# Host-side layout of the weights, larger DMA runs, and six smaller moves in a decoder-layer kernel

## The reference, cut to what matters

```python
a = rms_norm(h, norm_mix)
z, xbc, dt_raw, uv = split(a @ w_in)            # w_in: 1024 x 2568
y_ssd = gated_norm(ssd_scan(silu(conv(xbc)), softplus(dt_raw + dt_bias), ...), z)
u, v = split(gelu(uv)); y_gm = u * (tril(W_s) @ rms_norm(v) + b)
h = h + concat(y_ssd, y_gm) @ w_out             # 1024 x 1024
for e in range(16):                             # each token uses 2 of the 16 experts
    hid = silu(t @ w_gate[e]) * (t @ w_up[e])   # 1024 x 512 each
    y = y + comb[:, e:e + 1] * (hid @ w_down[e])  # 512 x 1024
h = h + y
h = h + sigmoid(rms_norm(h) @ w_pg) * rms_norm(p @ w_ple)
```

## Time and profile before

| | |
|---|---|
| median of three runs | 1130.89 us (1130.82 to 1131.54) |
| profiled execution: time, span | 1131.93 us, 1130.1 us |
| PE busy | 1057.6 us, 94% of the span |
| DVE, ACT, POOL busy | 700.2, 502.7, 184.1 us |
| DMA, mean | 181 GB/s, 204.82 MB |

### The profile page before, as it was taken

One profiled execution on the slowest core, in us unless ns is written; L12 is line 12 of the kernel. 1 busy time (PEld: TensorE's weight loads), 2 busy tenths in 40 slices (PEclk: granted clock), 3 DMA queues, 4 the chain that ended last, 5 costly groups with the idle time before them and its releaser, 6 DMA issues.

```text
span 1130.1 us, 17444 instructions
## 1 busy us (share of the span) xinstructions
PE 1057.6 (94%) x6221; PEld 912.5 (81%) x6222; DVE 700.2 (62%) x1103; ACT 502.7 (44%) x872; POOL 184.1 (16%) x344
## 2 busy tenths in 40 slices
PE   7999999997999999946999999799999999999896
PEld 5777799985776788745988999798899999878685
DVE  4422575814767667156599467889946753585664
ACT  6733322123111121151589357788935652564332
POOL 3611001100133112111000000000000000065542
PEclk9999999999899999857999999999999999999999
DMA  9701400222512362169399775999977556142441
GB/s 335 233 23 55 170 2 1 75 79 72 164 70 76 120 234 85 56 195 296 141 367 380 266 278 179 381 358 369 380 265 278 181 190 225 53 171 75 169 149 56
DMA packets 131607, 204.82 MB, mean 181 GB/s; under 512 B 11375, under 2 KB 98031, under 8 KB 131434
## 3 DMA queue, kind: packets, MB, share of 16 engines
q1 hardware_dynamic: 121450, 169.82, 44.2%
q0 software_dynamic: 6512, 21.77, 5.4%
q10 hardware_dynamic: 3600, 12.62, 2.8%
HBM read 169.74 MB, written 34.46 MB: 181 GB/s over the span
## 4 chain that ended last, share of the span: by engine, by line
PE 56%; DVE 10%; issue 4%; DMA 3%; ACT 2%; DVEq 1%; POOL 0%; ACTq 0%; SPq 0%; POOLq 0%; another core or an unknown queue 0%
PE bank L608 12%; PE bank L610 11%; PE bank L609 11%; PE bank L602 4%; DVE w_lo L1531 3%; PE bank L852 3%; PE bank L854 3%; PE bank L853 3%; PE bank L596 2%; PE bank L824 1%; PE bank L791 1%; DMA raw_gu<-in_w_up 1%; ACT w_hi L1923 1%; DMA xg<-m_rows,index_u 1%; DMA hx<-h_rows 1%
## 5 line engine op out<-in xcount | busy, mean ns | idle before, releaser
L608 PE MATMUL bank<-w_hi,xh 128*128 128x256 f32 x768 | 220.2, 287 | 2.7 <-DVE xl L1052 2.7
L609 PE MATMUL bank<-w_lo,xh 128*128 128x256 f32 x768 | 218.0, 284 | 0.0
L610 PE MATMUL bank<-w_hi,xl 128*128 128x256 f32 x768 | 218.0, 284 | 0.0
L1531 DVE SCALAR_TENSOR_TENSOR w_lo<-raw_gu,cols,w_hi 128x512 fp32r<-128x512 f32 x264 | 177.9, 746 | 10.9 <-ACT w_hi L1923 9.8
L1923 ACT ACTIVATE w_hi<-raw_gu,cols 128x512 fp32r<-128x512 f32 x264 | 165.4, 714 | 32.1 <-PE bank L610 16.4
L608 PEld LDWEIGHTS bank<-w_hi,xh 128*128 128x128 f32 x768 | 147.7, 192 | 4.2 <-issue 3.1
L609 PEld LDWEIGHTS bank<-w_lo,xh 128*128 128x128 f32 x768 | 147.9, 193 | 0.8
L610 PEld LDWEIGHTS bank<-w_hi,xl 128*128 128x128 f32 x768 | 147.7, 192 | 0.0
L608 PE MATMUL bank<-w_hi,hid_hi 128*128 128x512 f32 x192 | 79.6, 415 | 0.0
L2231 POOL COPY index_u<-token_u 128x1 uint32 (+1 forms) x25 | 6.1, 244 | 434.2 <-PE bank L602 411.5
L609 PE MATMUL bank<-w_lo,hid_hi 128*128 128x512 f32 x192 | 75.9, 395 | 0.0
(11 more groups left out here) (373 smaller groups left out, 2169.2 us busy)
## 6 DMA issues: line engine op xcount, KB each, us to landing
raw_gu<-in_w_gate SPq DMA_DIRECT2D x32, 1024.0 KB, 7.6
raw_gu<-in_w_up SPq DMA_DIRECT2D x32, 1024.0 KB, 10.1
raw_d<-in_w_down SPq DMA_DIRECT2D x16, 2048.0 KB, 11.8
y_rows<-yb ACTq DMA_DIRECT2D x24, 512.0 KB, 6.3
raw_w<-in_w_in SPq DMA_DIRECT2D x20, 512.0 KB, 6.3
xr<-in_x_prompt_t SPq DMA_DIRECT2D x8, 512.0 KB, 9.4
xst<-in_x_prompt SPq DMA_DIRECT2D x8, 512.0 KB, 9.7
raw_o<-in_w_out SPq DMA_DIRECT2D x8, 512.0 KB, 3.5
```

Of the source, the lines that this page charges most:

```text
L608: nc.tensor.matmul(out, lh(k), rh(k), start=(k == 0), stop=False)
L609: nc.tensor.matmul(out, lh(k), rl(k), start=False, stop=False)
L610: last = nc.tensor.matmul(out, ll(k), rh(k), start=False, stop=(k == (K or len(ks)) - 1))
L1531: ins = V.scalar_tensor_tensor(out=gu_lo[:, k, :, cols_], in0=raw_gu[q // KC][:, k, :, :], scalar=gain(e, k), in1=gu_hi[:, k, :, cols_].bi ...
```

## The change

- The host hands over `w_in`, gate and up, down and `w_pg` in the order in which they are loaded, so that a run is 4 KB (`w_in`) or 8 KB (gate, up, down, `w_pg`).
- Gate and up are loaded in four quarters of 1 MB (column half by half of the rows), down in two halves, each as soon as its part of the raw buffer has been split; ACT waits for each part by itself.
- All 16 blocks that could be unused are filled, in the first stage, behind the loads of the third block of `w_in`; the fills after the plan are gone.
- `p_in`, `ps_in` and the `norm_ple` row are loaded ahead of the expert stage; `p_in` has a place of its own.
- In a block `hid_transposes(1, ·)` comes behind the first quarter of down.
- The four low parts of the second half of `w_out` are made by POOL, ahead of its `y_rstd(0)`; ACT does `decay(0)` behind the first of the four high parts. `out_half(0, 0)` and the load of `s_nat` wait for POOL's semaphore `o_low`.

```diff
-                c0 = W_COLS[block]
-                sp.dma_start(raw_w[:, 2 * part:2 * part + 2, :], w_src[:, 2 * part:2 * part + 2, c0:c0 + BANK]
-                             ).then_inc(s(f"w{part}_loaded"), 16)
+                sp.dma_start(raw_w[:, 2 * part:2 * part + 2, :], i["w_in_blocks"][block, part]).then_inc(s(f"w{part}_loaded"), 16)
...
             for part in range(4):
                 w_load(2, part)
+            for b in range(NE, BLOCKS):
+                sp.dma_start(y_rows[b * P:(b + 1) * P, :].rearrange("p (k n) -> p k n", n=P),
+                             ones[:, :].unsqueeze(1).to_broadcast([P, KC, P])).then_inc(s("unused_filled"), 16)
...
-            sp.wait_ge(s("a_split"), KC * 5 + KC)
+            sp.wait_ge(s("o_low"), KC // 2)
...
-                for w, name in enumerate(("w_gate", "w_up")):
-                    sp.dma_start(raw_gu[q][:, :, w, :], i[name][0, bass.ds(e, 1), :, q * HE:(q + 1) * HE].rearrange(
-                        "o (k p) n -> p (o k) n", p=P)).then_inc(s(f"gu{q}_loaded"), 16)
+                sp.dma_start(raw_gu[q][:, part * KC // 2:(part + 1) * KC // 2].rearrange("p k w n -> p (k w n)"),
+                             i["w_gate_up"][bass.ds(e, 1), q, part].rearrange("o p n -> p (o n)")).then_inc(s(f"w{2 * q + part}_loaded"), 16)
...
+                if n == TILES + 1:
+                    sp.wait_ge(s("mTp_done"), TILES)
+                    sp.wait_ge(s("h_stored"), 16 * TILES)
+                    sp.dma_start(p_in, i["p_prompt_t"].rearrange("(k p) t -> p k t", p=P)).then_inc(s("p_loaded"), 16)
+                    sp.dma_start(ple_row, i["norm_ple"].partition_broadcast(P).rearrange("q o n -> q (o n)")).then_inc(s("c_rows_loaded"), 16)
...
-            with sp.If(unused > 0):
-                with sp.Fori(0, unused) as j:
-                    sp.dma_start(y_rows[bass.ds((BLOCKS - 1 - j) * P, P), :].rearrange("p (k n) -> p k n", n=P),
-                                 ones[:, :].unsqueeze(1).to_broadcast([P, KC, P])).then_inc(s("unused_filled"), 16)
...
-                gate_up(e, 0, sp.snap(done - KC - DC))
-                gate_up(e, 1, sp.snap(done - DC))
-                down(e, done)
+                for q in range(2):
+                    for part in range(2):
+                        gate_up(e, q, part, sp.snap(done - DC - (3 - 2 * q - part) * KC // 2))
+                down(e, 0, sp.snap(done - DC // 2))
+                down(e, 1, done)
...
                 b_rows(pe.snap(16 * n + 16))
-                hid_transposes(1, pe.snap(2 * n + 1))
                 pe.wait_ge(s("w_split"), steps + STEPS)
...
                 for quarter in range(4):
                     part, half = quarter // 2, quarter % 2
+                    if quarter == 1:
+                        hid_transposes(1, pe.snap(2 * n + 1))
...
             front(0)
-            for j in range(KC // 2):
-                o_split(1, j)
             weights(0)
...
             bt_evict(0)
-            for j in range(KC // 2):
+            o_high(1, 0)
+            decay(0)
+            for j in range(1, KC // 2):
                 o_high(1, j)
-            decay(0)
...
+            for j in range(KC // 2):
+                pool.wait_ge(s("a_high"), KC * 5 + KC // 2 + j + 1)
+                G.tensor_tensor(wo_lo[1][:, j, :], raw_o[:, j, :], wo_hi[1][:, j, :].bitcast(F32), ALU.subtract).then_inc(s("o_low"), 1)
             for n in range(TILES + 1):
                 if n < TILES:
                     y_rstd(n)
```

More of the change, by code:

```diff
@@ L61, in build @@
     TILES = NT + 1
-    IN = i["w_in"].shape[2]
+    IN = sizes["w_in"][2]
     HEADS = i["dt_bias"].shape[1]
@@ L77, in build @@
     EPG = NE // NG
-    DE = i["w_gate"].shape[3]
+    DE = sizes["w_gate"][3]
     DC = DE // P
@@ L518, in _ @@
                     sp.wait_ge(s("ssm_stored"), 16 * XC)
-                    gate_up(0, 0, None)
-                    gate_up(0, 1, None)
+                    for q in range(2):
+                        for part in range(2):
+                            gate_up(0, q, part, None)
                 if n == TILES:
@@ L525, in _ @@
                     sp.wait_ge(s("out_done"), 2 * TILES)
-                    down(0, None)
+                    for part in range(2):
+                        down(0, part, None)
+                if n == TILES + 1:
[3 more added lines that the diff above has]
+                    sp.dma_start(ple_row, i["norm_ple"].partition_broadcast(P).rearrange("q o n -> q (o n)")).then_inc(s("c_rows_loaded"), 16)
@@ L547, in _ @@
+                down(e, 0, sp.snap(done - DC // 2))
+                down(e, 1, done)
+            sp.wait_ge(s("lg_ready"), TILES)
             sp.dma_start(ps_in, i["p_sample_t"].rearrange("(k p) t -> p k t", p=P)).then_inc(s("p_loaded"), 16)
-            sp.dma_start(ple_row, i["norm_ple"].partition_broadcast(P).rearrange("q o n -> q (o n)")).then_inc(s("c_rows_loaded"), 16)
-            with sp.Fori(NE // 2, NE) as e:
+            with sp.Fori(1, NE) as e:
                 next_expert(e)
             for q in range(2):
[L553 to L556, removed]
+                for part in range(2):
+                    sp.wait_ge(s("w_split"), STEPS * NE - DC - (3 - 2 * q - part) * KC // 2)
+                    sp.dma_start(raw_gu[q][:, part * KC // 2:(part + 1) * KC // 2].rearrange("p k w n -> p (k w n)"),
+                                 i["w_pg_rows"][q, part]).then_inc(s(f"w{2 * q + part}_loaded"), 16)
@@ L557, in _ @@
+            sp.wait_ge(s("w_split"), STEPS * NE - DC // 2)
+            sp.dma_start(raw_d[:, 0:PC, :], i["w_ple"][0].rearrange("(k p) n -> p k n", p=P)).then_inc(s("d0_loaded"), 16)
             sp.wait_ge(s("w_split"), STEPS * NE)
-            sp.dma_start(raw_d[:, 0:PC, :], i["w_ple"][0].rearrange("(k p) n -> p k n", p=P)).then_inc(s("d_loaded"), 16)
             sp.dma_start(fin_row, i["norm_final"].partition_broadcast(P)).then_inc(s("c_rows_loaded"), 16)
@@ L1916, in split @@
                 x2 = isinstance(e, int)
-                if at[0] != "D":
-                    act.wait_ge(s(f"gu{int(at[0] == 'B')}_loaded"), 32 * (e + 1) if x2 else act.snap(32 * e + 32))
+                loads = {q * KC // 2: (f"w{q}_loaded", 7) for q in range(4)}
+                loads.update({2 * KC + q * DC // 2: (f"d{q}_loaded", 0) for q in range(2)})
                 steps = SPLITS[at]
                 for q in steps:
+                    if q in loads:
+                        name, earlier = loads[q]
+                        act.wait_ge(s(name), 16 * (e + earlier + 1) if x2 else act.snap(16 * e + 16 * earlier + 16))
                     if q < 2 * KC:
@@ L1951, in final_pg @@
             def final_pg(half, k):
-                if k == 0:
-                    act.wait_ge(s(f"gu{half}_loaded"), 32 * (NE + 1))
+                if k % (KC // 2) == 0:
+                    act.wait_ge(s(f"w{2 * half + 2 * k // KC}_loaded"), 16 * (NE + 8))
                 cols_ = slice(half * HE, (half + 1) * HE)
@@ L2327, with quarters @@
         arrays["state_ssm"][0].reshape(sizes["state_ssm"][1], -1, sizes["state_ssm"][4]).transpose(2, 0, 1))
+    w_in = arrays.pop("w_in")[0]
+    ssd, conv, heads, gm = sizes["ssd_norm"][1], sizes["conv_w"][2], sizes["dt_bias"][1], sizes["gmlp_norm"][1]
+    first = [ssd + conv + heads, ssd + conv + heads + gm, ssd + BANK, ssd, 0]
+    arrays["w_in_blocks"] = np.ascontiguousarray(
+        np.stack([w_in[:, c:c + BANK].reshape(-1, 2, p, BANK).transpose(0, 2, 1, 3) for c in first]))
+    arrays["w_in_dt"] = np.ascontiguousarray(w_in[:, ssd + conv:ssd + conv + heads].reshape(-1, p, heads).transpose(1, 0, 2))
+    n_e, de = sizes["w_gate"][1], sizes["w_gate"][3]
+    def quarters(pair):
+        both = np.stack(pair, axis=-2)
+        both = both.reshape(both.shape[:-3] + (2, d // p // 2, p, 2, 2, both.shape[-1] // 2))
+        both = np.moveaxis(both, (-2, -6, -4, -5, -3, -1), (-6, -5, -4, -3, -2, -1))
+        return np.ascontiguousarray(both.reshape(both.shape[:-3] + (-1,)))
+    arrays["w_gate_up"] = quarters((arrays.pop("w_gate")[0], arrays.pop("w_up")[0]))
+    w_pg = arrays.pop("w_pg")[0]
+    arrays["w_pg_rows"] = quarters((w_pg[:, :BANK], w_pg[:, BANK:]))
+    w_down = arrays.pop("w_down")[0].reshape(n_e, 2, de // p // 2, p, d)
+    arrays["w_down_rows"] = np.ascontiguousarray(w_down.transpose(0, 1, 3, 2, 4).reshape(n_e, 2, p, -1))
     arrays["p_prompt_t"] = np.ascontiguousarray(arrays.pop("p_prompt")[0, 0].T)
```

49 lines of the change are left out of this document (21 added, 28 removed).

## The result

The changed kernel takes 1127.3 us (median), and the kernel before, timed again beside it, 1132.5; the ratio is 0.9945, 95% interval 0.9929 to 0.9962, or 6.2 us less (4.3 to 8.0). One of the seven runs of the changed kernel took 1690.3 us at a granted clock of 0.64, and the ratio leaves it out. The forecast was 1123.7 us, that is 0.9936 of the 1130.89 measured earlier, with 7.2 us gained. The profiled execution has a span of 1124.2 us where the kernel before had 1130.1: 5.9 us less.

The account below looks back on a forecast made before the run. PE, busy for 94% of the span, was taken as the bound, so its waits were priced: 0.1 + 1.3 + 2.8 + 3.0 = 7.2 us gained, 1123.7 us on the median's scale. The range was 1115 to 1128.5 us.

Parts of the forecast that it names:

- The sum: Whole kernel: start 0.1, head 1.3, gather 2.8 and expert stage 3.0 us, together 7.2 us gained, 1123.7 us.
- The signs: Expected traces: nine PE waits of about 1.3 us at line 608, no 0.50 clock in the expert stage, gather 4 to 5 us.
- The load of p_in: Expert stage, block at 731 us: moving the load ends a 4.9 us wait and 2.4 us of half clock, 7.3 gained.
- Rival E: Expert stage: 8 KB runs not faster, quarters queue, an equal wait comes up elsewhere; 1131.0 us, chance 0.05.
- The order: Expert stage: a quarter of down enters each late block's cycle, 19.9 us against PE's 18.6; nine waits, 4.3 us cost.
- Rival C: Expert stage: loads made all nine late splits, so with loads a block ahead all those waits go; 1112.0 us, chance 0.10.
- The head: SSD stage's head: DVE and POOL take turns, 1.3 us gained; ends are 5.3 gained without blocking and 1.2 lost.
- A: SSD stage's head: DVE isn't held by POOL, its instructions go back to back; 4.0 us more, 1119.7 us, chance 0.17.
- B: SSD stage's head: POOL keeps the port through all its subtractions; 1.2 us lost instead of 1.3 gained, 1126.2 us, chance 0.13.
- The gather and the fills: Ahead of the first expert block: gather without fills beside it gains 2.8 us, between 1.4 and 3.5; first-stage fills free.
- The rest: Larger runs at the very start gain 0.1 us, at most 0.3; ACT's additional load waits per expert cost nothing.
- Rival D: First stage: fills hold up SP's queue, the fourth block of w_in is late, PE stands; about 1138 us, chance 0.05.

Follow-up runs that it names:

- e3: The kernel before with only p_in, ps_in and the norm_ple row loaded at their new place, ahead of the expert stage; ratio 0.9947 to the kernel before.
- e2: The changed kernel with p_in, ps_in and the norm_ple row loaded between experts 7 and 8 again; ratio 0.9937 to the kernel before.
- e10: e2 with quarters of gate and up issued only once their whole half is split, halves of down once all is; ratio 0.9931 to the kernel before.
- e1: The changed kernel with hid_transposes(1) put back ahead of the first quarter of down; ratio 0.9914 to the kernel before.
- e6: The changed kernel with the four low parts back on DVE, behind cat_low(0), and PE waiting where it reads them; ratio 0.9945 to the kernel before.
- e8: The changed kernel with eight fills after the plan again, ACT waiting ahead of the expert stage only for the first stage's eight; ratio 0.9985 to the kernel before.
- e4: The changed kernel with eight of the sixteen fills after the plan again, ACT still waiting for all fills; ratio 1.0082 to the kernel before.

## Why the prediction was right, point by point

**The sum.** 7.2 us forecast, 6.2 measured (4.3 to 8.0), 5.9 in the profile; 1123.7 us is 0.9936 of the time before, within the measured interval. That the total came out closer than its parts is partly luck: the head gave 0.9 us less than forecast and the first block took 1.0 more, the start and the expert stage gave 0.5 more each. e3, the kernel before with nothing but the three loads moved, is at 0.9947, as fast as the whole change; what the gather and the head gave, the new order took. Two slips carry no weight: the upper end of the range adds up to 0.1 - 1.2 + 1.4 + 1.0 = 1.3 us gained, 1129.6 and not 1128.5, and ACT waited three times per expert in the kernel before, not four. The signs came as named: PE's waits moved to the first down matmul, nine of them, 1.2 to 1.5 us each; no granted clock of 0.50 behind the first block until 980 us; the gather 4.8 us.

**The load of p_in.** 7.3 us forecast, 6.7 measured in e3. The prediction said that the price of long runs matters where a load ends a wait, and named this block as the place; but it left that price open and gave the whole wait to the new place of `p_in`. e2 and e10 show that the new loads alone remove it too. The same 7 us was removed twice, and the sum came out right only because it had given the loads nothing. Rival E, whose first premise was that 8 KB runs are not faster, is wrong in that premise.

**The order.** 4.3 us of cost forecast, 3.5 measured in e1 between the rows, 4.0 by the waits (11.6 less 7.6); where the half microsecond between the two lies isn't shown. The cycle of 19.9 us was right (from the wait at 705.21 to the next at 725.06 it is 19.85). The old order without the load I took at 7.4 us of waits in nine blocks; it has 7.6 in e1 and in e3. The two errors, 0.6 for the load and 0.8 for the order, nearly cancel, which is luck: 6.7 - 3.5 = 3.2 us against the 3.0 of the sum, and 3.5 between the rows. Rival C is out: with the loads a block ahead, all nine waits are there.

**The head.** 1.3 us forecast, 0.4 measured. The choice between the ends was right for this place: turns, one POOL instruction each; A (no blocking) and B (POOL keeps the port) are both out by the durations 2.84 and 2.83 us. Mis-sized were two terms. `xwd` was left out: POOL's first subtraction starts at 272.00 us and stretches it to 1.50, where it takes 0.69 in e6, without POOL; `weights(0)` starts 0.6 us later for it than forecast. And the subtraction takes 2.35 us where it goes first and 8.36 / 3 = 2.8 where it takes turns, while I took 2.0 from four instructions with another operand form; that makes the turns 0.3 us longer. The Trainium skill ("GPSIMD Engine Reference", section "Elementwise — side-by-side cycle accounting") gives 4.497 us for a `tensor_tensor` of 2048 fp32 columns, 2.2 for half of it as an estimate; the trace's 2.35 us agrees. As an upper price of no contention, e6's 5.1 us beyond the change, 5.6 beyond the kernel before, meets the 5.3 of the upper end.

**The gather and the fills.** 2.8 us forecast, 2.9 measured. The first stage's fills were free: SP from 50.07 us for 27.47, 1.7 us each against 1.5 forecast, and ACT began on the fourth block of `w_in` at 114.25 us. Not foreseen: the first block took 1.0 us more, which looks like a part of the gather's gain given back. It is the clock. Busy time by stretch, 523 to 526 us (length, PE, PEld, DVE, ACT, POOL, PEclk, DMA share, GB/s), in the kernel before, the changed kernel and e3:

```profile
523.00:526.00 3.00, 3.00 (x21) 3.00 (x21) 3.00 (x6) 0.02 (x1) 0.00 (x0) 0.75 0.62 223
```

```profile
523.00:526.00 3.00, 3.00 (x26) 3.00 (x26) 3.00 (x3) 0.38 (x1) 0.00 (x0) 0.95 1.01 374
```

```profile
523.00:526.00 3.00, 3.00 (x16) 3.00 (x16) 3.00 (x5) 0.00 (x0) 0.00 (x0) 0.50 0.75 265
```

TensorE is granted 0.50, its 1.2 GHz, from 520 to 523 us in all three. It starts on the first expert's weights at 521.48, 517.63 and 521.74 us, and its matmuls are twice as fast from 524.4, 523.3 and 527.9 us: 2.9, 5.7 and 6.1 us later. e3 has the gather of the kernel before, with the fills beside it (9.03 us of wait), and yet its first block takes 536.26 - 517.04 = 19.2 us, longer than the change's 19.0. So the 1.0 us isn't the price of an earlier gather: the clock came back early in the one profile of the kernel before.

**The rest.** The start gained 0.6 us instead of 0.1: PE's first matmul starts 0.3 us earlier, and the matmuls, 0.43 us apart at first, are 0.23 apart from 11.3 us instead of 12.5 (the column of the granted clock shows 1.00 there in both). e1, with the same first stage, starts its first matmul as early, has them 0.23 apart from 12.9 us, and begins the SSD stage at 270.35, as the kernel before. So the loads gained nothing that lasts, and the 0.6 us belongs to the one execution. Rival D didn't occur.

## What to carry to other kernels

Two parts of a change may remove the same wait: price what each does alone before they are added, for the second is then worth nothing, or can be left out. When the late engine and the engine that waits are not the same, moving the wait of the second is no gain if it puts the first one's next input behind more work. When a step is moved to a later place or to a slower engine, look at every queue in which something stands behind its completion: most of the 5 us won in the head was lost again to one load on SP.

## What the runs showed of the hardware

Where several loads queue, long runs also free the engine that issues them: behind `p_in` SP stood up to 4.08 us in one issue with runs of 1 KB, and 0.36 us in one with runs of 8 KB.

The place of the half-clock stretches changes between executions whose work there is the same. The changed kernel and e1 do the same work up to the expert stage, yet from 462 to 468 us they show (busy time by stretch, first the change, then e1):

```profile
462.00:468.00 6.00, 5.23 (x12) 4.14 (x13) 0.72 (x2) 0.00 (x0) 1.68 (x1) 0.50 0.22 89
```

```profile
462.00:468.00 6.00, 4.37 (x26) 3.67 (x26) 1.53 (x3) 2.02 (x4) 2.85 (x4) 1.00 0.40 161
```

From 332 to 338 us it is the other way round, 1.00 in the change and 0.66 to 0.77 in e1. e8's profile is granted 0.50 from 353 to 362 us, where the change's has 1.00: one tile took 382.04 - 351.50 = 30.5 us in e8's and 25.5 in the change's, 5 us by the clock alone. e4, which like e8 has eight fills less in the first stage, shows the same stretch, so that one may go with the edit. But the twelve timed runs of e8 alone reach from 1127.6 us, at a mean granted clock of 0.969, to 1136.4 at 0.962, and its profile is of the longest. The Trainium skill ("TensorE: Matmul & The Clock Gate", Part 1) says that the phase of the clock's control against the kernel's start differs from run to run. The change and e1 agree with that, with matmuls 0.23 us apart from 11.3 and from 12.9 us; e2, which has the same first stage too, is at 11.4, and what sets the phase isn't shown here. For a kernel of this kind a single profile can be off by some microseconds, and a small gain is to be read from the stage that it is in, with the timed ratio beside it.
